# Joint products at the start of two gated groups, another product order and earlier token sums in a Winograd feed-forward stage

## The reference, cut to what matters

```python
def conv_ffn(h, prev, w_up, conv_w, conv_b, w_down):
    l = h.shape[1]
    u = h @ w_up                       # 1024 -> 2 x 2816
    ext = jnp.concatenate([prev, u], axis=1)
    y = conv_b + sum(conv_w[k] * ext[:, k:k + l] for k in range(CONV_WIDTH))
    a, v = jnp.split(y, 2, axis=-1)
    return (jax.nn.silu(a) * v) @ w_down, ext[:, -(CONV_WIDTH - 1):]
```

## Time and profile before

| what | value |
|---|---|
| median of 3 runs | 2983.37 us (2981.18 to 2990.52) |
| the profiled execution, its own time | 2988.75 us |
| its span, first to last instruction | 2986.9 us |
| PE busy | 2789.5 us, 93% |
| DVE busy | 1853.9 us, 62% |
| ACT busy | 1230.3 us, 41% |
| POOL busy | 1224.4 us, 41% |
| mean granted TensorE clock | 0.965 |

### The profile page before, as it was taken

How to read it: one execution, slowest core, us unless ns; L and a number is a source line. 1 busy time by engine, 2 the same in 40 slices (tenths; PEclk the granted TensorE clock), 3 DMA queues, 4 the chain that set the end, 5 groups by cost and what they waited for, 6 DMA issues and landing times. The chain is left out here.

```text
span 2986.9 us, 54773 instructions
## 1 busy us (share of the span) xinstructions
PE 2789.5 (93%) x21032; PEld 2562.2 (86%) x21032; DVE 1853.9 (62%) x3420; ACT 1230.3 (41%) x2492; POOL 1224.4 (41%) x788
## 2 busy tenths in 40 slices
PE   8998979999989997999999889899987999998998
PEld 8996966666767796999999889887887999997898
DVE  6212248888545526877776866695347777767665
ACT  5002027777723314445544433314235454544332
POOL 4430000000000143555555878560325555557886
PEclk9999989999989998999999999999998999998999
DMA  6216750000357420122222322313111222232322
GB/s 188 56 42 231 227 181 16 2 2 2 107 165 222 126 92 24 66 86 80 74 84 98 103 93 70 126 49 117 43 42 47 84 69 84 69 102 101 110 80 87
DMA packets 168199, 272.16 MB, mean 91 GB/s; under 512 B 19702, under 2 KB 112220, under 8 KB 166768
## 3 DMA queue, kind: packets, MB, share of 16 engines
q1 hardware_dynamic: 141636, 225.19, 23.0%
q10 hardware_dynamic: 26316, 43.66, 4.5%
HBM read 226.22 MB, written 46.69 MB: 91 GB/s over the span
## 5 line engine op out<-in xcount | busy, mean ns | idle before, releaser
L3092 PE MATMUL banks<-token_blocks_high,weight_blocks_high 128*128 128x272 f32 x3584 | 754.0, 292 | 87.4 <-issue 51.3
L3092 PE MATMUL banks<-token_blocks_high,weight_blocks_low 128*128 128x272 f32 x3584 | 745.9, 291 | 0.0
L3092 PE MATMUL banks<-token_blocks_low,weight_blocks_high 128*128 128x272 f32 x3584 | 745.3, 290 | 0.0
L3092 PEld LDWEIGHTS banks<-token_blocks_high,weight_blocks_high 128*128 128x128 f32 x3584 | 567.9, 191 | 96.3 <-issue 70.0
L3092 PEld LDWEIGHTS banks<-token_blocks_low,weight_blocks_high 128*128 128x128 f32 x3584 | 569.8, 191 | 0.0
L3092 PEld LDWEIGHTS banks<-token_blocks_high,weight_blocks_low 128*128 128x128 f32 x3584 | 566.9, 191 | 0.0
L2987 POOL TENSOR_TENSOR weight_blocks_low<-ight_quarters_more,weight_blocks_high 128x512 fp32r<-128x512 f32 (+2 forms) x152 | 233.4, 1536 | 162.6 <-ACT weight_blocks_high L3116 162.4
L3364 DVE SCALAR_TENSOR_TENSOR conv_space<-conv_space,conv_w 128x1024 f32<-128x1024 f32 x176 | 235.9, 1340 | 73.4 <-ACT conv_space L3169 62.3
L2987 POOL TENSOR_TENSOR weight_blocks_low<-weights_whole,weight_blocks_high 128x512 fp32r<-128x512 f32 (+2 forms) x146 | 214.3, 1469 | 154.6 <-ACT weight_blocks_high L3116 154.3
L2987 POOL TENSOR_TENSOR weight_blocks_low<-weights_again_whole,weight_blocks_high 128x512 fp32r<-128x512 f32 (+2 forms) x146 | 214.9, 1474 | 152.3 <-ACT weight_blocks_high L3116 152.1
L3402 DVE TENSOR_TENSOR x<-x,banks 128x544 f32<-128x544 f32 x224 | 160.9, 719 | 158.0 <-PE banks L3092 154.1
(11 more groups left out here) (509 smaller groups left out, 5525.7 us busy)
## 6 DMA issues: line engine op xcount, KB each, us to landing
gated_scratch<-conv_space ACTq DMA_DIRECT2D x44, 544.0 KB, 3.7
past_rows<-in_kv_pages SPq DMA_DIRECT2D x160, 128.0 KB, 2.4
ight_quarters_more<-in_w_up SPq DMA_DIRECT2D x56, 256.0 KB, 2.9
weights_whole<-in_w_up SPq DMA_DIRECT2D x56, 256.0 KB, 3.1
weights_again_whole<-in_w_up SPq DMA_DIRECT2D x56, 256.0 KB, 3.0
staged<-gated_scratch SPq DMA_DIRECT2D x16, 816.0 KB, 6.6
z<-in_kv_pages SPq DMA_DIRECT2D x96, 128.0 KB, 2.5
x<-in_cmp_pages ACTq DMA_DIRECT2D x64, 128.0 KB, 5.6
```

The lines of the kernel that those rows point to most:

```text
L3092: last = pe.matmul(out[:, piece, :], a[:, at], b[:, kk, piece * HP:(piece + 1) * HP], start=first and kk == 0 and z == 0, stop=kk == n - 1 ...
```

## The change

The order of the sequence, the placing of the PSUM sets and the order on the queues change; the arithmetic and the number of matmuls do not.

1. Token sums: DVE interleaves the scaling and lowering of the first tokens differently, makes the two sums that need no product first (`SUM_ORDER` 3, 4, 2, 6), then the other two directly after them; the four lowerings follow, the one for block 6 after the first convolution of unit 0. ACT rounds the sums ahead of and between the weight blocks.
2. ACT's copies of unit 0 and the first copy of unit 1 stand before the taps of unit 0.
3. `copy(LAST, "V1")` stands before both taps of unit 20 and not after them.
4. Groups 0 and 1 of the down half start with joint products of their first two units, (22,0) (23,0) (22,1) (23,1) and (26,0) (27,0) (26,1) (27,1). POOL makes three weight sums after product 1 and the fourth after product 3.
5. All down units run their products in the order 0, 1, 3, 2, 5, 4, 6; DVE's drain between two adds to the same tokens moves from product 4 to product 5 with it. The PSUM sets of the units come from a table (`SETS`), in which the joint units use one set for B and E.
6. The convolution and gate of unit 21, the staging of group 1 and the sums and lowerings for group 1 come at other places: lowerings of blocks 0 and 1 after i = 19 and 20 (before 15 and 16), sums after i = 21 to 24 (before 18, 20, 21, 23).

```diff
+SUM_ORDER = (3, 4, 2, 6)
+DOWN_ORDER = (0, 1, 3, 2, 5, 4, 6)
+GATED_ORDER = (3, 2, 4, 6), (3, 4, 6, 2)
+JOINT_PARTS = (0, 1)
...
+        DOWN_LEADS = tuple(FC + PER * p for p in JOINT_PARTS)
+        def joint(q, order):
+            return [(u, j) for j in order[:2] for u in (q, q + 1)] + [(u, j) for u in (q, q + 1) for j in order[2:]]
+        SEQUENCE = [(q, j) for q in range(1, LEAD) for j in range(BLOCKS)] + joint(LEAD, range(BLOCKS))
+        for q in range(FC, UNITS):
+            if q in DOWN_LEADS:
+                SEQUENCE += joint(q, DOWN_ORDER)
+            elif q - 1 not in DOWN_LEADS:
+                SEQUENCE += [(q, j) for j in DOWN_ORDER]
...
-                eng.wait_ge(x_added, BLOCKS * (q - FC) + ("V1", "C11", "V2", "V5", "C22", "C12", "C21").index(what) + 1)
+                eng.wait_ge(x_added, place_of(q, ("V1", "C11", "V2", "V5", "C22", "C12", "C21").index(what)) - BLOCKS * LAST + 1)
...
-                elif q == FC + 2:
+                elif q == FC + 3:
                     stage(1)
...
+            for q, j in SEQUENCE:
+                lower(q, j)
+                if q == 1 and j == 1:
                     second_sums(1)
+                elif (q, j) == (LEAD, BLOCKS - 1):
+                    first_sums(LAST)
+                    second_sums(LAST)
+                elif q >= FC and q - 1 not in DOWN_LEADS:
+                    if j == 1:
+                        first_sums(q)
+                        third_sum(q)
+                    elif j == 3:
+                        fourth_sum(q)
+                    elif j == 6 and q in DOWN_LEADS:
+                        first_sums(q + 1)
+                        third_sum(q + 1)
+                elif q >= FC and j == 3:
+                    fourth_sum(q)
...
             copy_first("C11")
             copy_first("C21")
+            round_sum(3)
             round_weights(0)
             round_weights(1)
-            round_sum(3)
+            round_sum(4)
             round_sum(2)
-            act.wait_ge(constants_loaded, 16 * 3)
             round_weights(2)
+            round_sum(6)
             round_weights(3)
-            round_sum(4)
             copy_first("C12")
             copy_first("C22")
+            copy(1, "V1")
+            round_weights(4)
+            act.wait_ge(constants_loaded, 16 * 3)
             tap(0, 0)
+            round_weights(5)
             tap(0, 1)
-            round_sum(6)
...
+                if q == LEAD and j == 5:
+                    copy(LAST, "V1")
                 if j == 5:
                     tap(q, 0)
                 elif j == 6:
                     tap(q, 1)
-                if q == LEAD and j == 6:
-                    copy(LAST, "V1")
...
             difference(x1, x2, x1, made)
+            dve.tensor_tensor(x2, x4, x2, ALU.subtract).then_inc(made, 1)
             wait_product(dve, 0, 5)
             difference(t2_raw, x4, x1, made)
-            difference(x2, x4, x2, made)
-            dve.drain()
-            lower(2)
-            lower(3)
-            lower(4)
             difference(x3, x3, t2_raw, made)
-            lower(6)
+            for j in (2, 3, 4):
+                lower(j)
...
                     if av == 0:
                         place(1, "C11")
+                        lower(6)
...
-            for j in (3, 4, 2, 6):
+            for j in GATED_ORDER[0]:
                 gated_sum(0, j)
-            lower_gated(0, 2)
             for p in range(len(PAIRS)):
                 for i in range(PER * BLOCKS):
-                    add(FC + p * PER + i // BLOCKS, i % BLOCKS)
+                    add(*at_place(BLOCKS * (LAST + p * PER) + i))
+                    for j, at in zip(DOWN_ORDER[2:], (2, 2, 3, 4, 5)) if p == 0 else zip(DOWN_ORDER[5:], (0, 1)):
+                        if i == at:
+                            lower_gated(p, j)
                     if p == 0:
-                        for (av, tap), at in zip(((0, 1), (0, 0), (1, 1), (1, 0)), (3, 4, 5, 6)):
+                        for (av, tap), at in zip(((0, 1), (0, 0), (1, 1), (1, 0)), (6, 7, 8, 10)):
                             if i == at:
                                 convolve(LAST, av, tap)
-                        if i == 8:
+                        if i == 11:
                             gate(LAST)
-                    for j, at in zip(range(3, BLOCKS), (0, 1, 2, 2)) if p == 0 else zip((5, 6), (0, 1)):
-                        if i == at:
-                            lower_gated(p, j)
                     if p + 1 < len(PAIRS):
-                        early = (15, 16, 18, 20, 21) if p == 0 else (9, 11, 12, 14, 16)
-                        late = (23, 25, 26, 27) if p == 0 else (21, 23, 24, 25)
+                        early = (19, 20, 21, 22, 23) if p == 0 else (9, 11, 12, 14, 16)
+                        late = (24, 25, 26, 27) if p == 0 else (21, 23, 24, 25)
```

More of the change, by code:

```diff
@@ L2777, in feed_forward @@
         block = ctx.enter_context(nc.Block())
-        JOINT = [(0, 0), (1, 0), (0, 1), (1, 1)] + [(u, j) for u in range(2) for j in range(2, BLOCKS)]
         LEAD, FIRST_PRODUCTS, FIRST_BLOCKS = LAST - 1, 8, 4
@@ L2841, in ring @@
             return f.ring(FIRST_BLOCKS + place_of(q, j), width(q) * P)
-        def bank_set(q, which):
-            a, b, e = ((3 * (q - 1) + i) % 4 for i in range(3))
-            if q == LEAD:
-                e = b
-            elif q == LAST:
-                a, b, e = bank_set(LEAD - 1, "E"), bank_set(LEAD - 1, "B"), bank_set(LEAD, "B")
-            return (a, b, e)["ABE".index(which)]
+        SETS = {q: tuple((3 * (q - 1) + i) % 4 for i in range(3)) for q in range(1, LEAD)}
+        SETS[LEAD] = SETS[LEAD - 2][2], SETS[LEAD - 1][0], SETS[LEAD - 1][0]
+        SETS[LAST] = SETS[LEAD - 1][2], SETS[LEAD - 1][1], SETS[LEAD][2]
+        for q in range(FC, UNITS):
+            (_, _, e2), (a1, b1, e1) = SETS[q - 2], SETS[q - 1]
+            if q == FC:
+                SETS[q], SETS[q + 1] = (b1, SETS[LEAD][0], SETS[LEAD][0]), (e1, a1, a1)
+            elif q in DOWN_LEADS:
+                SETS[q], SETS[q + 1] = (e2, e1, e1), (b1, a1, a1)
+            elif q - 2 in DOWN_LEADS:
+                SETS[q] = e2, a1, SETS[q - 2][0]
+            elif q - 1 not in DOWN_LEADS:
+                SETS[q] = e2, a1, b1
+        def bank_set(q, which):
+            return SETS[q]["ABE".index(which)]
         def bank(q, which):
@@ L3238, in _ @@
                     tap(q, 1)
-                if q == LEAD and j == 6:
-                    copy(LAST, "V1")
                 if q == LAST and j in (2, 3):
                     round_gated(0, j - 2)
-            for j in range(2, BLOCKS):
+            for j in DOWN_ORDER[2:]:
                 round_gated(0, j)
@@ L3302, in _ @@
             norm_rows(0, rows[3])
+            dve.wait_ge(gained, 1)
             lower_rows(0, rows[2], 3)
+            norm_rows(1, halves[0])
             lower_rows(0, rows[3], 4)
-            dve.wait_ge(gained, 1)
-            halves = (slice(0, 2), slice(2, 4))
-            for t in range(1, 4):
-                if t == 2:
-                    dve.wait_ge(spreaded, 2)
-                norm_rows(t, halves[0])
-                norm_rows(t, halves[1])
+            norm_rows(1, halves[1])
+            lower_rows(1, halves[0], KH + 1)
+            dve.wait_ge(spreaded, 2)
+            norm_rows(2, halves[0])
+            lower_rows(1, halves[1], KH + 2)
+            norm_rows(2, halves[1])
+            norm_rows(3, halves[0])
+            norm_rows(3, halves[1])
+            for t in (2, 3):
                 lower_rows(t, halves[0], KH + 2 * t - 1)
@@ L3445, in _ @@
                             lower_gated(p + 1, 1)
[L3446 removed]
+                        for j, at in zip(GATED_ORDER[1], (*early[2:], late[0])):
                             if i == at:
                                 gated_sum(p + 1, j)
[L3449 removed]
+                        for j, at in zip(DOWN_ORDER[2:5], late[1:]):
                             if i == at:
```

75 lines of the change are left out of this document (34 added, 41 removed).

## The result

| kernel | median | runs | ratio to before, 95% interval |
|---|---|---|---|
| before | 2987.1 us (2981.18 to 2990.52) | 6 | |
| after | 2992.88 us (2988.18 to 2995.69) | 6 | 1.0024 [1.0013, 1.0035] |

The change makes the kernel 0.24% slower: 5.8 us between the medians, 4 to 10 by the interval. By the bound of the prediction (0.3%) that is "the same", and 2992.88 lies in the range of 2967 to 3004; the forecast was 2987. The profiled execution took 2989.8 us, its span is 2987.9. The two feed-forward stages in it are 2.8 and 4.0 us longer than before; the rest of the program, which no edit touches, is about 6 us shorter in this pair of executions, so their own times (2989.8 and 2988.75) lie closer than the medians. One execution of an experiment, the profiled one of "the product order alone", ran at a mean granted clock of 0.83, took 3204 us and is left out of that kernel's ratio.

What follows compares the result with a forecast made beforehand. PE, busy 93%, bounds the kernel; only its standstills and half clock, about 65 us a stage, can be won. Terms sum to +2.5 and +1.8, together +4.3 on the median of 2983.37: 2987.7, rounded to 2987; range 2967 to 3004.

Steps and rivals of the forecast that it cites:

- A: Unit 1, seven products: sums in a row and copies ahead of taps start (1,2) earlier, 7.3 us less a stage.
- B: End of unit 20 and unit 21 but for the first down product: early copy saves 6.3 us, first stage 5.0.
- C: First 14 down products: DVE late with sums, lowerings and adds, 1.6 us more a stage.
- D: Next 14 down products: group 1's lowerings and sums crowd DVE, 7.6 us more, first stage 7.9.
- E: First 4 products of group 1: joint start finds POOL ready, 5.6 us less, first stage 6.6.
- F: Other 24 products of group 1: waits on DVE and one clock dip, 5.2 us more, first stage 3.9.
- G: Group 2 of the down half: waits before product 6, 3.9 us more a stage.
- H: Group 3 and the tail: four waits before product 6 less earlier excess, 3.4 us more a stage.
- slower by the clock: Rival: long new PE waits bring half-clock dips, some 6 us more a stage, 2999 us; chance 0.27.
- DVE keeps up: Rival: DVE's sums overlap less with POOL, unit 25's waits vanish, about 8 us a stage less, 2971; chance 0.23.
- hidden: Rival: the wait before product 6 costs nothing in the down units, 38 us less, 2950; chance 0.04.
- A gives little: Rival: POOL and DVE slow each other more, (1,2) comes only 4 us earlier, 2994 or 2996; chance 0.10.

Runs made afterwards that it cites:

- the product order alone: Kernel before with only the down products reordered to 0, 1, 3, 2, 5, 4, 6: 3014.59 to 3019.95 us, ratio 1.0111.
- the run with the one-step sum: Kernel after with the two-step gated sum of groups 1 to 3 made in one step, so part of the output differs: 2973.14 us, ratio 0.9959.
- the up-half kernel: Kernel before with only the up half's changes (scaling order, token sums in a row, copies ahead of taps): 2956.5 us, ratio 0.9905.

## Why the prediction was right, and where its steps were off

Each stretch against its forecast, in us, second feed-forward (first):

| stretch | predicted | measured |
|---|---|---|
| first unit, before A | 0 (0) | -4.4 (-4.0) |
| A | -7.3 (-7.3) | -5.8 (-6.2) |
| B | -6.3 (-5.0) | -6.3 (-5.1) |
| C | +1.6 (+1.6) | +1.1 (-0.5) |
| D | +7.6 (+7.9) | +7.6 (+8.4) |
| E | -5.6 (-6.6) | -5.6 (-6.3) |
| F | +5.2 (+3.9) | +8.8 (+6.8) |
| G | +3.9 (+3.9) | +4.3 (+5.7) |
| H | +3.4 (+3.4) | +4.2 (+4.2) |
| sum | +2.5 (+1.8) | +4.0 (+2.8) |

(The sums are of unrounded lengths, with 0.2 less for the up loop of the first stage.)

- **What was right.** The change is two edits of opposite sign: the up half gains 28 to 30 us (the kernel with it alone), the down half gives more than all of it back. PE stands before product 6 in all 16 units, 0.86 to 0.94 where DVE is free, and (1,2), (21,2) and the start of group 1 show what was foretold of them (6.98 us ended by POOL, none, none). The waits in unit 25 and before (28,4) and (29,6) are where the walk through DVE's queue put them. The copy of unit 21 is worth its 6 us of B. E hit to a tenth in the second stage, for the reason given.
- **D and C, right in size and partly by luck.** D hit to a tenth, but of other parts. The four waits on DVE were priced at 9.0 with their restarts and stood for 6.5 (0.91, 0.89, 2.67, 2.00), about 7.5 with them. A wait of 0.68 on POOL and 2.2 us lost at the half clock, where 1.6 was counted, filled the rest. In C the forecast had DVE late at (22,3) and (22,6); four of the five waits in the trace are ended by POOL, 2.68 before (23,1), which was not foreseen, and 3.90 before (22,3). The +1.1 for +1.6 is a near miss by another engine's queue.
- **The scaling reorder, costed at nothing with bounds of ±1.** It brought the first sum 3.2 us forward in the second stage and 1.3 in the first. The prediction took it for the same set of operations and gave it nothing. In the earlier trace rows one sees that an operation of DVE beside POOL is slow, and the same view some 15 us earlier would have shown two lowerings of DVE beside POOL's first weight sums (4.47 us for the two). In the new order the operations that read PSUM stand there.
- **A.** POOL's chain of five was walked right (17.0 against 17.3), and ended 3.3 us sooner for that reorder. (1,2) came 11.6 us earlier against PE's first product of the stage, 7.9 was predicted. Of this 1.4 was lost again before (1,6): the lowering of block 6 between the convolutions took 3.41 beside POOL and not 2.4, and (1,2) ran slower (5.32 against 4.57). First unit and A together: -10.1, predicted -7.3.
- **F, the term most mis-sized.** The five waits that were priced at 10.0 with their restarts stood for 8.8, about 10.1 with 0.26 of restart each (1.18 less 0.91 in unit 24). But one dip of 1.6 was counted, and the clock of 0.93 over 68.9 us is 4.8 lost (4.6 by the durations of the products). So the rival "slower by the clock" was right on F, and on C and D, where the lengths came out as forecast, its extra cost did not appear. The run with the one-step sum shows it: without the 2.24 the clock is 0.98 and 5.6 us come back.
- **The waits of product 6.** 1.2 us each was right (1.18 in unit 24). Alone on the kernel before, the order costs 1.04 a unit net. In the kernel after, taking it back gave 17 us only. The order's 33 us, the joint starts' 18 and the up half's -29 would make +22, and the total is +6. The 16 us between are about what E differs by: with the joint starts it takes 9.1 (9.3) in the new order and 16.9 (17.7) in the old, 16.2 us in both stages. The prediction had E's 9.0 right and did not say that it hangs on the product order.
- **POOL's first two sums, put at nothing.** The change moves them behind the lowering for product 1 in every down unit but the joint ones that follow. In the natural order that costs 1.6 to 1.9 us of G; what it costs in the kernel after is not shown.
- **The rivals.** "DVE keeps up" (2971) and "hidden" (2950) are refuted by the trace. "A gives little" went the other way. The sum came out near because errors cancel, which is luck. F, G and H are 4.8 us over the forecast in the second stage and 5.4 in the first; first unit and A are 2.8 and 2.9 under. And the forecast stood on the median of 2983.37, where more runs of the kernel before gave 2987.1: +4.3 was predicted and +5.8 measured. The "about 65 us a stage" of the prediction's first paragraph add up to 61 by its own list; nothing rests on it.

The Trainium skill (SBUF — State Buffer, "SBUF: two separate sides") bears on the missed step: its lock concerns a DVE operation with two SBUF inputs, or one in a two-port mode, against GpSimd. A scaling operation of DVE has one input in PSUM. The trace agrees: three of them take 3.67, the first beside POOL's sum of 2.25, and 3.67 in the first stage too, where POOL stands. The lowerings, with two SBUF inputs, took 4.40 for two beside the same POOL operations in the old order. As an exclusive lock it also gives the POOL row, by estimate: that sum starts at 2221.83 while DVE's lowering runs to 2222.92, 1.1 us of waiting and 1.3 of work (its time alone), 2.4 against the 2.25 measured.

## What to carry to other kernels

Take an edit of two signs apart before it is judged: here one half was worth 1% and the other cost more, and the sum looked like nothing. A product that adds into a bank which the vector engine reads needs another product in between, 1.2 us a time here. And walk the vector engine's queue with the durations that its operations have beside GpSimd, also for a mere reorder: which of two operations meets GpSimd moved the first sum here by 3.2 us in one stage and 1.3 in the other.

## What was not expected of the hardware

- In the kernel after, a standstill of PE of 2.0 to 2.9 us was followed by 0.7 to 1.5 us of lost cycles in the product behind it ((25,4) 3.17, (28,4) 3.92, (29,6) 4.02 instead of 2.49), the waits of 0.86 to 0.94 by none (2.47 to 2.50); so in the second stage. The length of the one standstill doesn't decide it. In the first stage 0.91 before (25,6), which followed 2.66 before (25,4), had a product of 4.38 behind it. And in the kernel before, 2.33 before (28,2) and 2.24 before (28,5) were followed by products of 2.35 and 2.31, which lost nothing. One DVE operation of 2.5 us less ahead of such a wait gave 5.6 us in F (5.1 in the first stage).
- Executions of one kernel differ in where the half clock falls: the up-half kernel had 15.7 and 13.7 us for E of the first stage in its two profiles, 47.8 and 48.9 for C. Gains of under 3 us in one stretch can't be read from one profile.
